# Mixture of experts on one core: tokens as the stationary operand, w1 and w3 split into high and low parts, groups added back inside the loop

## The reference

```python
def grouped_moe(u, w_router, b_router, w1, w3, w2):
    scores = sigmoid(t @ w_router); sel = scores + b_router
    ...   # best group by the sum of its two best sel; the two best experts in it
    gates = ...   # (tokens, 16), two of them not zero, sum 1
    h = silu(einsum('td,edf->tef', t, w1)) * einsum('td,edf->tef', t, w3)
    y = einsum('tef,efd->td', h * gates[..., None], w2)
```

## Time and profile before

| | us |
|---|---|
| median of 3 runs | 921.64 |
| lowest, highest | 910.05, 921.74 |
| the profiled execution | 919.88 |
| its span, first to last instruction | 917.8 |
| TensorE busy, matmuls | 808.1 |
| VectorE busy | 418.0 |
| ScalarE busy | 173.5 |
| GpSimd busy | 36.4 |

### The profile page before, as it was taken

The page is one execution under the profiler, slowest core; times in us unless marked ns, Lnnn a source line. Parts: engine busy times, 40 slices in busy tenths (PEclk is TensorE's granted clock), DMA queues, the critical chain, the costliest instruction groups (busy, mean ns, idle before and its releaser), DMA issues.

```text
span 917.8 us, 12490 instructions
## 1 busy us (share of the span) xinstructions
PE 808.1 (88%) x4920; PEld 671.6 (73%) x4922; DVE 418.0 (46%) x792; ACT 173.5 (19%) x357; POOL 36.4 (4%) x32
## 2 busy tenths in 40 slices
PE   1399988979699888998996999897997999999995
PEld 1399875769587777777846998675885888888862
DVE  6797885436565433443048465344363011111106
ACT  0344523300230000000014354241022200000000
POOL 3000000001200000000001000000010000000001
PEclk8579998999599999999995899999986999999998
DMA  9969987100179988898730564720000267777731
GB/s 357 370 216 355 352 299 301 44 1 1 47 229 346 389 344 349 347 377 342 280 105 13 158 186 141 299 114 1 1 18 29 92 275 275 278 286 291 294 132 47
DMA packets 71902, 192.34 MB, mean 210 GB/s; under 512 B 9383, under 2 KB 41383, under 8 KB 63659
## 3 DMA queue, kind: packets, MB, share of 16 engines
q1 hardware_dynamic: 66024, 184.73, 53.8%
q10 hardware_dynamic: 5830, 6.94, 2.4%
HBM read 190.60 MB, written 1.05 MB: 209 GB/s over the span
## 4 chain that ended last, share of the span: by engine, by line
PE 79%; DVE 7%; DMA 5%; issue 4%; POOL 1%; ACT 1%; SPq 1%; DVEq 1%; POOLq 0%; ACTq 0%
PE bank L1645 23%; PE bank L1678 11%; PE bank L1362 10%; PE bank L1360 6%; PE bank L1546 6%; DMA e_ring<-in_w 4%; PE bank L1629 4%; PE bank L1325 3%; PE bank L1693 1%; PE bank L1561 1%; PE bank L1481 1%; PE bank L1662 1%; PE bank L1491 1%; PE bank L1440 1%; DMA ada_open<-in_w_ada 1%
## 5 line engine op out<-in xcount | busy, mean ns | idle before, releaser
L1645 PE MATMUL bank<-arena,e_ring 128*128 (+1 forms) x2048 | 240.9, 280 | 15.1 <-DMA e_ring<-in_w 7.8
L1645 PEld LDWEIGHTS bank<-arena,e_ring 128*128 128x128 f32 x2048 | 237.6, 196 | 17.2 <-issue 17.0
L1678 PE MATMUL bank<-e_ring,arena 128*128 128x512 f32 x256 | 115.3, 593 | 2.3 <-DVE arena L1226 2.3
L761 DVE SCALAR_TENSOR_TENSOR mod_acc<-ada_ring,c_col,mod_acc 128x1024 f32<-128x1024 f32 x66 | 83.3, 1282 | 62.9 <-DMA ada_ring<-in_w_ada 62.4
L1221 DVE TENSOR_TENSOR arena<-arena,bank 128x256 f32<-128x256 f32 x32 | 13.4, 418 | 167.4 <-PE bank L1662 167.4
L1678 PEld LDWEIGHTS bank<-e_ring,arena 128*128 128x128 f32 x256 | 46.2, 190 | 48.5 <-issue 48.5
L1362 PE MATMUL bank<-w_hi,u_hi 128*128 128x256 f32 (+2 forms) x224 | 68.3, 305 | 7.9 <-DVE u_lo L874 7.2
L712 ACT ACTIVATE arena<-bank 128x256 f32<-128x256 f32 x32 | 12.3, 383 | 322.6 <-PE bank L1645 322.6
L1362 PE MATMUL bank<-w_lo,u_hi 128*128 128x256 f32 (+2 forms) x224 | 67.7, 302 | 0.0
L1362 PE MATMUL bank<-w_hi,u_lo 128*128 128x256 f32 (+2 forms) x224 | 67.5, 301 | 0.0
L853 DVE TENSOR_TENSOR w_lo<-w_ring,w_hi 128x2048 fp32r<-128x2048 f32 (+2 forms) x24 | 52.1, 2179 | 18.4 <-ACT w_hi L534 18.3
(11 more groups left out here) (240 smaller groups left out, 1011.7 us busy)
## 6 DMA issues: line engine op xcount, KB each, us to landing
e_ring<-in_w SPq DMA_DIRECT2D x96, 1024.0 KB, 7.7
ada_ring<-in_w_ada SPq DMA_DIRECT2D x66, 512.0 KB, 6.4
w_ring<-in_w_in SPq DMA_DIRECT2D x20, 1024.0 KB, 5.5
ada_open<-in_w_ada SPq DMA_DIRECT2D x30, 512.0 KB, 9.0
w_ring<-in_w_out SPq DMA_DIRECT2D x8, 1024.0 KB, 6.4
w_ring<-in_w_in SPq DMA_DIRECT2D x2, 1056.0 KB, 5.6
ln_gb<-in_ln_g ACTq DMA_DIRECT2D x4, 512.0 KB, 5.6
ln_gb<-in_ln_b ACTq DMA_DIRECT2D x4, 512.0 KB, 6.9
```

The costliest lines, as they stand in the source:

```text
L761: V.scalar_tensor_tensor(out=part, in0=ada_open[slot][:], scalar=k_col, in1=part, op0=ALU.mult, op1=ALU.add).then_inc(ada_free, 1)
L1645: mm = pe.matmul(bank[j % 2][:, (2 * q + c) * CAP:(2 * q + c + 1) * CAP], w[:, k, c * P:(c + 1) * P], moving, start=(k == 0), stop=(k == K ...
L1678: mm = pe.matmul(bank[4 + half][:, :], hT[:, j % 2, c * CAP:(c + 1) * CAP], w[:, c, half * 512:(half + 1) * 512], start=(j == 0 and c == 0 ...
```

## The change

- **w1 and w3.** The sorted tokens are now the stationary operand (128 slots), and w1 and w3 together the moving one, 512 columns at a time. Each expert's w1 and w3 come as two chunks (one half of the 1024 rows each, 1 MB). ScalarE makes the high part of a chunk (`up_high`, into one of three slots), VectorE the low part in place (`up_low`). The sorted tokens stand there as a high and a low part too (`us_hi`, `us_lo`). `expert_up` makes 24 fp32r products per expert.
- **Hidden tile.** The product comes out with the tokens on partitions, so the gate is one number per partition: `gates_to_slots` makes all 16 at once, `group_gate` is gone, `hidden` is one instruction. `turn_hidden` turns the result (two transposes), and ScalarE copies it to `hT`. w2 stays in float32 (`expert_down`).
- **Sorting.** The normalised tokens are split into `xn_hi` and `xn_lo`, and `sort_tokens` makes two passes. It stands ahead of the branch on `crowded`, so the masks do too.
- **Adding back.** `scatter(g)` runs for each group once its four experts are done, from a high and a low part of the group's result (`yg_hi`, `yg_lo`).
- **Buffers.** One ring of 10 slots holds w_in's tiles, their high parts, w_out's tiles, the chunks (5 slots), their high parts (3) and w2 (2). Layer 1's w_in tiles have 7 slots.
- **w_ada of the next layer.** Six tiles are gathered while w_out is multiplied, then three with each expert; the bias and the zeroing of the accumulator are moved ahead in two parts. The loops over experts are written out.
- `ones` is now a part of `ident_mask`, filled after that has been copied.

```diff
-W_SLOTS = 4
...
+N_SLOTS = 10
+W_RAW = ((0, 1, 2, 3), (6, 7, 3, 8, 4, 5, 9))
+W_HIGH = ((7, 8, 9), (2, 0, 1))
+E_RAW = (4, 5, 6, 7, 3)
+E_HIGH = (0, 1, 2)
+E_DOWN = (8, 9)
+N_CHUNKS = 2 * N_EXP
...
+ADA_NEXT = [(k, m) for k in range(KC) for m in (0, 1, 2, 5)] + [(k, m) for k in range(KC) for m in (3, 4)]
+ADA_EARLY = 4 * KC
+ADA_STEP = 3
+ADA_AHEAD = 2
+ADA_STEPS = ADA_TILES // ADA_STEP
...
+            def load_up(l, c):
+                Y = layer_view(l)
+                slot, e, h = E_RAW[c % len(E_RAW)], c // 2, c % 2
+                if c >= len(E_RAW):
+                    sp.wait_ge(*Y(chunk_done, c - len(E_RAW) + 1))
+                dst = e_ring[slot][:].rearrange("p (q k f) -> p q k f", q=2, f=F_EXP)
                 for q, name in enumerate(("w1", "w3")):
...
+                    sp.dma_start(dst[:, q, :, :], a[name].rearrange("l e (p k) f -> l e p k f", k=KC)[
+                        l, e, :, h * KC // 2:(h + 1) * KC // 2, :]).then_inc(slot_in[slot], 16)
+            def load_down(l, e):
+                if e >= 2:
+                    sp.wait_ge(*layer_view(l)(down_done, e - 1))
+                slot = E_DOWN[e % 2]
+                sp.dma_start(e_ring[slot][:].rearrange("p (c n) -> p c n", c=2),
+                             a["w2"].rearrange("l e (c p) n -> l e p c n", p=P)[l, e]).then_inc(slot_in[slot], 16)
...
+                if l == 0:
+                    sp.wait_ge(ada_free, ADA_OPEN + ADA_TILES)
+                sp.wait_ge(*Y(w_free, NW_IN))
+                for c in range(len(E_RAW) - 1):
+                    load_up(l, c)
+                for e in range(2):
+                    load_down(l, e)
+                for step in range(ADA_AHEAD):
+                    load_next_ada(l, step)
+                sp.wait_ge(*Y(mix_done, 2 * W_OUT_TILES))
+                load_up(l, len(E_RAW) - 1)
+                for e in range(N_EXP):
+                    for c in (2 * e + 5, 2 * e + 6):
+                        if c < N_CHUNKS:
+                            load_up(l, c)
+                    load_next_ada(l, ADA_AHEAD + e)
+                    if 2 <= e + 1 < N_EXP:
+                        load_down(l, e + 1)
...
+            def up_high(l, c):
+                Y = layer_view(l)
+                act.wait_ge(*arrivals["up", l, c])
+                slot = E_HIGH[c % len(E_HIGH)]
+                if c < len(E_HIGH):
+                    act.wait_ge(*Y(mix_done, W_OUT_TILES + 1 + slot))
+                else:
+                    act.wait_ge(*Y(chunk_done, c - len(E_HIGH) + 1))
+                nc.scalar.activation(e_hi[slot][:], e_ring[E_RAW[c % len(E_RAW)]][:], ACT.Copy).then_inc(e_hi_ready, 1)
...
+                for c in range(len(E_HIGH)):
+                    up_high(l, c)
+                def norm_high(t):
+                    act.wait_ge(*Y(xn_ready, t + 1))
+                    nc.scalar.activation(xn_hi[:, t, :], xn[:, t, :], ACT.Copy).then_inc(xn_hi_ready, 1)
+                norm_high(0)
                 evict_x(4, 1)
+                norm_high(1)
...
+                for k in range(KC):
+                    act.wait_ge(*Y(sorted_done, k + 1))
+                    nc.scalar.activation(us_hi[:, k, :], bank[k][:, :], ACT.Identity, bias=mcol[:, 1, 0, k:k + 1],
+                                         scale=mcol[:, 1, 1, k:k + 1]).then_inc(us_hi_out, 1)
...
+                    for e in range(N_EXP):
+                        act.wait_ge(*Y(chunk_done, 2 * e + 2))
+                        silu_out(e, 0 if e == 0 else 4)
+                        if e == 0:
+                            act.wait_ge(M.turned_back, 1)
+                            nc.scalar.activation(from_slot[:, 0, :], bank[6][:, :], ACT.Copy).then_inc(M.from_act, 1)
+                        if 2 * e + 3 < N_CHUNKS:
+                            up_high(l, 2 * e + 3)
+                        if e % 4 == 0 and e > 0:
+                            group_out(e // 4 - 1)
+                        turned_out(e)
+                        if 2 * e + 4 < N_CHUNKS:
+                            up_high(l, 2 * e + 4)
...
+            def up_low(l, c):
+                dve.wait_ge(*layer_view(l)(e_hi_ready, c + 1))
+                slot = E_RAW[c % len(E_RAW)]
+                V.tensor_tensor(e_lo[slot][:], e_ring[slot][:], e_hi[E_HIGH[c % len(E_HIGH)]][:].bitcast(F32),
+                                ALU.subtract).then_inc(e_lo_ready, 1)
...
+                for step in range(ADA_AHEAD):
+                    next_ada(step)
+                def norm_low(t):
+                    dve.wait_ge(*Y(xn_hi_ready, t + 1))
+                    dve.wait_ge(*Y(xt_done, (NT + t + 1) * KC))
+                    V.tensor_tensor(xn_lo[:, t, :], xn[:, t, :], xn_hi[:, t, :].bitcast(F32), ALU.subtract).then_inc(xn_lo_ready, 1)
...
+                        norm_low(0)
...
+                up_low(l, 0)
+                norm_low(1)
+                up_low(l, 1)
...
+                for k in range(KC + 1):
+                    if k < KC:
+                        dve.wait_ge(*Y(us_hi_out, k + 1))
+                        V.scalar_tensor_tensor(out=us_rest[:, k, :], in0=bank[k][:, :], scalar=mcol[:, 1, 1, k:k + 1],
+                                               in1=us_hi[:, k, :].bitcast(F32), op0=ALU.mult,
+                                               op1=ALU.subtract).then_inc(us_diff, 1)
+                    if k > 0:
+                        dve.wait_ge(*Y(us_diff, k))
+                        V.tensor_scalar(us_lo[:, k - 1, :], us_rest[:, k - 1, :], mcol[:, 1, 0, k - 1:k], None,
+                                        ALU.add).then_inc(us_lo_out, 1)
+                choose_experts()
+                up_low(l, 2)
...
+                def hidden(step, gate, b):
+                    dve.wait_ge(M.silu_done, step + 1)
+                    if step:
+                        dve.wait_ge(M.h_turned, step)
+                    V.scalar_tensor_tensor(out=hid[:], in0=silu[:], scalar=gate, in1=bank[b][:, F_EXP:2 * F_EXP],
+                                           op0=ALU.mult, op1=ALU.mult).then_inc(M.h_ready, 1)
...
+                    for e in range(N_EXP):
+                        hidden(e, gates_s[:, e:e + 1], 0 if e == 0 else 4)
+                        if e == 0:
+                            dve.wait_ge(M.turned_back, 2)
+                            V.tensor_copy(from_slot[:, 1, :], bank[7][:, :]).then_inc(M.from_dve, 1)
+                        if 2 * e + 3 < N_CHUNKS:
+                            up_low(l, 2 * e + 3)
+                        if e % 4 == 0 and e > 0:
+                            group_out(e // 4 - 1)
+                        if 2 * e + 4 < N_CHUNKS:
+                            up_low(l, 2 * e + 4)
+                        next_ada(ADA_AHEAD + e)
...
+                    for q, part in enumerate((xn_hi, xn_lo)):
+                        for t in range(NT):
+                            mm = pe.matmul(bank[k][:, :], part[:, t, k:k + KC * (P - 1) + 1:KC], to_slot_r[:, t, :],
+                                           start=(q == 0 and t == 0), stop=(q == 1 and t == NT - 1))
+                    mm.then_inc(sorted_done, 1)
...
+            def expert_up(l, e, tile, b, step, first, done):
+                if step > 1:
+                    pe.wait_ge(M.h_ready, step)
+                if e == 0:
+                    pe.wait_ge(*Y(us_lo_out, KC))
+                    pe.wait_ge(*Y(us_hi_out, KC))
+                dst = bank[b][:, :].rearrange("p (q f) -> p q f", q=2)
+                cols = slice(tile * CAP, (tile + 1) * CAP)
+                for h in range(2):
+                    c = 2 * e + h
+                    hi, lo = [w[:].rearrange("p (q k f) -> p q k f", q=2, f=F_EXP)
+                              for w in (e_hi[E_HIGH[c % len(E_HIGH)]], e_lo[E_RAW[c % len(E_RAW)]])]
+                    if first:
+                        pe.wait_ge(*Y(e_hi_ready, c + 1))
+                    for k in range(KC // 2):
+                        for q, u in enumerate((us_hi, us_lo)):
+                            pe.matmul(dst, u[:, h * KC // 2 + k, cols], hi[:, :, k, :], start=(h == 0 and k == 0 and q == 0),
+                                      stop=False)
+                    if first:
+                        pe.wait_ge(*Y(e_lo_ready, c + 1))
+                    for k in range(KC // 2):
+                        mm = pe.matmul(dst, us_hi[:, h * KC // 2 + k, cols], lo[:, :, k, :], start=False,
+                                       stop=(h == 1 and k == KC // 2 - 1))
+                    if done:
+                        mm.then_inc(chunk_done, 1)
...
+            def turn_hidden(step):
+                pe.wait_ge(M.h_ready, step + 1)
+                for c in range(2):
+                    mm = pe.transpose(bank[5][:, c * P:(c + 1) * P], hid[:, c * P:(c + 1) * P], ident)
+                mm.then_inc(M.h_turned, 1)
+            def expert_down(l, e, step, banks, start, stop, signal):
+                pe.wait_ge(*arrivals["down", l, e])
```

(40 more changed lines are left out.)

577 lines of the change are left out of this document (226 added, 351 removed).

## The result

| | before | changed |
|---|---|---|
| median, us | 921.64 (3 runs) | 864.26 (4 runs) |
| lowest, highest | 910.05, 921.74 | 862.69, 872.75 |
| profiled execution, its span | 919.88, 917.8 | 862.69, 860.8 |
| TensorE / VectorE / ScalarE busy | 808.1 / 418.0 / 173.5 | 717.2 / 565.1 / 309.4 |

The ratio is 0.9442 (95% interval 0.9395 to 0.9490): faster by 5.6%, at 864.3 us where 862 was forecast. That close agreement is partly luck, as will be seen. The page of the changed kernel first: the busy totals, then two of the lines with 40 slices of 21.5 us.

What follows compares the result with a forecast made beforehand. TensorE was taken to bound layer 1's experts, bytes and late-freed slots layer 0's. From the profiled 919.9 us, 31 us less in layer 1 and 27 in layer 0 gave 862 us, range 846 to 889.

Steps and rivals of the forecast that it cites:

- layer 1's stretch: Layer 1, sort's start to VectorE taking the first token tile's second half (the mark): 31 us less than 202.1.
- layer 0's: Layer 0, same stretch, bound by DMA bytes at 11.5 us per expert: 197 us, 27 us less with the late start.
- Period: Layer 1's expert loop, time per expert: 8.86 us on TensorE plus 0.1 us of semaphore time, where it was 11.03.
- Turn back and gates: Once-only work in layer 1's stretch, 16 tiny gate records and 8 transposes on TensorE: 2.7 us.
- The 512-column product: TensorE's w1/w3 work per expert: 0.2155 us per fp32r product, 24 of them 5.2 us, 5.7 at the upper end.
- rival (d): Consecutive 512-column products overlap, from 0.164 us down, so DMA bounds layer 1: 19 us less, 843 us; chance 0.04.
- (b): Weight load doesn't hide under 512 columns: 0.325 us a product, 11.9 us an expert, 915 us; chance 0.08 with smaller causes.
- The end: Layer 1 after the last expert, up to the mark: last hT copy, output split and 4 products, 2.4 us.
- Adding back early: Three groups added back within the loop for 5.2 us on TensorE; before, 8 float32 products (6.88 us) preceded VectorE's second half.
- rival (c): Expert loops: the weight split closes into one loop, 13.4 us per expert, slower, about 958 us in total; chance 0.05.
- Ahead of the sort: Work moved before each layer's sort, mainly low parts on VectorE, starts the sort later: +1.5 us per layer.
- rival (a): Layer 0's DMA stays at 354 to 368 GB/s, 13.1 us per expert: 876 to 885 us, say 881; chance 0.18.

Runs made afterwards that it cites:

- e1: The changed kernel run once more with nothing edited: 871.88 us, expert stretches 201.0 us in layer 0 and 174.6 us in layer 1.
- e9: The changed kernel run again unedited, as yardstick for the kernels beside it: median 869.97 us of 4 runs, ratio to the kernel before 0.9452.
- e4: Changed kernel with all adding-back products after the last expert, output wrong, only time read: median 867.66 us, ratio to the kernel before 0.9487.
- e10: Changed kernel with all adding back after the last expert, results right, kept in dead columns of the sorted tokens: ratio to the kernel before 0.9367.

## Why the prediction was right, and where it was off

**The direction and the mechanism** held: TensorE is the bound of layer 1, the bytes that of layer 0, the split hides under both. The forecast was 169.4 us for layer 1's stretch (13.5 + 155.9) and 197 for layer 0's (its terms, 45 + 3 x 9.3 + 9 x 11.5 + 9.2 + 10.6, make 196.2); measured 174.6 to 175.4 and 201.0 to 202.7. So 4 to 6 us too few in each, some 10 in all. The rest of the span was to grow by 3 us to 493.4; e1 and e9 have 494.3 and 493.3. Their totals are 872. That the profiled execution came out at 862.69 is luck: 8 us of clock in the two projections, for which no term of mine stood. The median of 864.26 is near the forecast probably for the same reason (e9's is 869.97), but its other executions have no trace.

**Layer 1, term by term.** To the first expert 12.3 us for 13.5: -1.2. Period 9.13 for 8.96: +2.7. Turn back and gates 0.87 + 1.68 for 2.7, clock 1.9 for 2.2 (the first expert's products take 7.4 us for 5.5): -0.5. Three scatters 5.5 for 5.2: +0.3. A stall after the second expert, 5.6 us (697.10 to 702.74) for 3.9 us of products: +1.8, and 0.1 in that expert's own products. At the end, beside w2's usual 3.4 us, 0.8 for the last hidden tile's copy and a slow start of w2, then 4.3, for 2.4: +2.7. Together +5.9; measured 175.4 - 169.4 = 6.0.

**The 512-column product** was the term mis-sized in the price of every expert: I took 0.2155 us, half of w2's record; it is 0.228 (5.48 us for 24), within the bounds I had. In the sum of layer 1 this is 16 x 24 x 0.0125 = 4.8 us. The 0.1 us per expert that I charged for semaphores doesn't show, which takes 1.6 us off; with the rounding the 2.7 above are left. The Trainium skill ("TensorE: Matmul & The Clock Gate", "Back-to-back issue gap") has 131 ns for a sustained stream of such pairs; here it is 228, and rival (d) falls with it. So does (b): the loads of weights hide.

**The end** was a step left out: before, VectorE's first half ran under the second half's products (6.88 us for eight); now the second half's products run under VectorE's first half, which takes 2.1 us itself (842.55 to 844.62). My 2.4 us stopped ahead of it.

**Adding back early** was sized nearly right in the loop (5.5 us for 5.2), but what it replaces was taken from the old kernel: 6.9 us of float32 products. The same fp32r products at the end cost 1.4 us (e4) or nothing (e10). So this part of the change gives away 5.5 us in layer 1, beside the order of e10; in layer 0 no difference shows.

**The stall** is rival (c)'s shape, once per layer. ScalarE's timeline, then VectorE's:

```profile
697.35 0.38 ACT L811 ACTIVATE hT<-bank 128x256 f32<-128x256 f32 x1 [5.56 <-PE bank L1725]
697.63 1.90 ACT L620 ACTIVATE e_hi<-e_ring 128x2048 fp32r<-128x2048 f32 x1
699.43 0.38 ACT L806 ACTIVATE silu<-bank 128x256 f32<-128x256 f32 x1
```

```profile
699.56 2.29 DVE L969 TENSOR_TENSOR e_lo<-e_ring,e_hi 128x2048 fp32r<-128x2048 f32 x1 [4.55 <-ACT e_hi L620]
701.77 0.47 DVE L1355 SCALAR_TENSOR_TENSOR hid<-silu,rt,bank 128x256 f32<-128x256 f32 x1
```

The second expert's products had ended by 697.1 us, but the first hidden tile's transposes stand behind them on TensorE, the copy of the transposed tile behind that on ScalarE, then a chunk's high part, and only then the second SiLU, which is done at 699.8. VectorE had waited for that high part and makes its low part first, so the second hidden product comes at 701.77. TensorE has w2's eight products meanwhile, which is why the loss is 1.8 us and not 5. From then on the experts' order gives the split its spare time, as forecast.

**Ahead of the sort** +1.3 us for +1.5.

**Layer 0.** Turns of 11.52 us at 409 GB/s, as forecast (11.5 at 411): rival (a)'s gaps didn't come. The Trainium skill's 358 GB/s ("DMA: Bandwidth & Descriptors", "Where 436 GB/s comes from") would be 13.2 us a turn; here, where one core runs, the trace disagrees for 100 us on end. What was off is how soon this pace begins: I let three experts run on what was loaded ahead, at 9.3 us, before nine at 11.5. One did: from the second hidden product to the fourteenth the intervals are 9.0, 12.7, and ten near 11.5 (one of 12.4, one of 11.9), 138.1 us for 131.4. A w_ada step stands ahead of each hidden product in VectorE's queue and its slots hold one step, so the loads pace VectorE from the third expert on (the chain has its wait of 8.55 us for a tile at 291.00), though chunks are in hand: from 300 to 400 us ScalarE never waits for one. The second expert's w2 came 44.0 us after the sort's start for the forecast's 45, the fourteenth's 137.2 us later for 131.4, and from there to the mark it took 21.5 for 19.8, late at the end as in layer 1.

## What to carry to other kernels

Price a moved piece of work against the same work left in its place, not against the old version: in the last microseconds, products that fill another engine's wait are free. Where transfers are consumed in lockstep with the computation, one step a turn, taking one away helps only if it leaves a turn that the bytes bound. And compare stretches, not totals: here they repeat to 1 or 2 us, while the clock moves a total by 8.

## What was not expected of the hardware

- TensorE's granted clock under an unchanged, busy stretch had two courses in 14 executions: 288 products in 35.4 to 35.8 or 39.2 to 40.0 us, 336 products in 41.1 to 41.5 or 45.1 to 45.5, with nothing between, and in the slow course a second fall from 2.4 to 1.2 GHz after the first rise, though the engine stays busy.
- An fp32r product of 512 columns takes 0.228 us, one of 256 columns 0.1185. From these two it is 0.43 ns a column and 0.009 us fixed, an estimate.
- One core read 409 to 411 GB/s from the chip's memory for 100 us in transfers of 512 KB and 1 MB, with ScalarE and VectorE reading and writing SBUF all the time.
